# A three-block network in fp32 pairs: late low parts on GpSimd, two units' high products first, forget gate sums in the level loop

## The chip, the cores and the metric

One core of a Trainium2 chip runs one program. The metric is the device time of one execution in microseconds (us). Before: a median of 2212.71 us over 3 executions (2212.23 to 2213.28).

## What is computed

The input is one sequence of 512 tokens of width 1024. The first block is a token mixer of four recurrences and attentions, cross attention over 256 memory tokens and a gated network; two further layers follow. The change touches only the first mixer's beginning:

```python
xn = rmsnorm(x, norm_mix_pre)          # x * rsqrt(mean(x*x) + eps) * gain
proj = xn @ w_in + b_in                # 1024 -> 3592 columns
(m_q, m_k, m_v, m_o, m_i, m_f, ..., h_q, h_f, h_i, h_g) = split(proj)
# mlstm: log_f = log_sigmoid(m_f), g = cumsum(log_f), limits from i - g
# hgrn:  f = lb + (1-lb)*sigmoid(h_f), log_f = log f, g = cumsum(log_f),
#        attn[t,s] = sum_k q[t,k] exp(g[t,k]-g[s,k]) k[s,k]
```

## The kernel before

**Units.** Every matrix is cut into units of 128 output columns: 1024 x 128 weights, 512 KB, in a ring of four buffers (`raw`, `wh`, `wl`). For each unit SyncE's queue loads `raw`, ScalarE writes the rounded high part `wh` (L1377), GpSimd subtracts to get the low part `wl` in two halves (L523), and TensorE makes 24 products of 128x128 by 128x512: high by `xh`, high by `xl`, low by `xh` for each of the eight blocks of x. VectorE then empties the PSUM bank (`scaled`, L1951), which also applies the token norm. ScalarE adds the bias. `unit_split`, `unit_done` and `emptied` count these steps. ScalarE makes the high parts where the program text calls `raise_to(n)`, so what stands ahead of such a call delays the unit.

**The start.** ScalarE makes `xh` from the eight blocks of x (L1758), VectorE `xl` (`low`, L1951), and TensorE's first unit waits for each block of `xl` in turn. Before, the first four units go one at a time: 16 high products (L1103, L1104), then 8 low ones (L1110). Ahead of unit 1's low products stand the token sums of the norm (L680), which need the squares made by ScalarE (L1765) and added by VectorE (L2021, L2023). After unit 1 the inverse root is spread over the partitions (L698), and only then is unit 0's bank emptied. Units 4, 5 and 6 follow (L591 to L593); unit 4's high part waits for that first emptied bank, unit 6's comes after ScalarE's gate functions in `hgrn` (L1610 to L1617).

**The recurrence's levels.** `hgrn` works on two halves b of 128 channels. For each it runs seven levels and a diagonal: VectorE makes an argument (`level_argument`, L2235 and L2236), ScalarE its exponential (L1633), VectorE the operands (`level_operands`, L2241), TensorE the scores of all heads (16 small products, L1021) and then one whole unit (`fill`) to have work meanwhile. VectorE also copies the level's scores out (L2275) and empties the unit. VectorE's work in a level stands in this order: argument, scores of the level before, operands, emptying of the unit. The next scores wait for the operands.

**The forget gates.** These are rows of 4x512 for the other recurrence (`mlstm`). ScalarE takes a logarithm (`gate_logarithms`, L1538 to L1541), VectorE sums and bounds (`forget_sums`, `gate_rows_made`, `gate_limits`, L2142 to L2159, all ahead of the levels), TensorE turns the rows into columns (L983), and ScalarE copies the columns to `small` (L1649). Ahead of the levels TensorE waits for this copy (`take(cols_ready)`).

Of the kernel before, what the change touches and what calls it, by code (L numbers as in the profile page):

```python
# [30 lines left out]
P = 128  # L31
# [150 lines left out]
def build(nc, x_in, mem_in, w_in, par_in, con_in, moba_in, alibi_in, na_in, dist_in, out):  # L182
    with ExitStack() as ctx:
# [313 lines left out]
        @block.sync  # L497
        def _(sp):
            sp.dma_start(par[:], par_in).then_inc(inputs_in, 16)
            for b in (0, 2, 4, 5, 6, 7):  # L500
                sp.dma_start(x[:, b, :], x_in[:, b, :]).then_inc(x_in_sem[b], 16)
            for k in range(1, RING):
                sp.dma_start(raw[:, k, :], w_in[k * P:(k + 1) * P, :]).then_inc(unit_in[k], 16)
                if k == 1:
                    sp.dma_start(con[:, 0:EARLY_CONSTS], con_in[:, 0:EARLY_CONSTS]).then_inc(early_constants_in, 16)
            sp.dma_start(con[:, EARLY_CONSTS:], con_in[:, EARLY_CONSTS:]).then_inc(constants_in, 16)
            with sp.Fori(1, UNITS // RING) as i:
                for k in range(RING):

                    sp.wait_ge(unit_done, RING * i + (k + 1 - RING))  # L510
                    sp.dma_start(raw[:, k, :], w_in[bass.ds((RING * i + k) * P, P), :]).then_inc(unit_in[k], 16)
            for n in range(UNITS // RING * RING, UNITS):
                sp.wait_ge(unit_done, n + 1 - RING)
                sp.dma_start(raw[:, n % RING, :], w_in[n * P:(n + 1) * P, :]).then_inc(unit_in[n % RING], 16)


        @block.gpsimd
        def _(pool):
            def lower(k, high):
                pool.wait_ge(high_split, high)  # L520

                for half in (slice(0, KT * P // 2), slice(KT * P // 2, KT * P)):
                    m = pool.tensor_tensor(wl[:, k, half], raw[:, k, half], wh[:, k, half].bitcast(F32), ALU.subtract)  # L523
                m.then_inc(unit_split, 1)

            for w in weights:
                m = pool.memset(w, 0.0)
            m.then_inc(weights_cleared, 1)
            for n in range(RING):
                lower(n, n + 1)  # L530
            with pool.Fori(1, UNITS // RING) as i:  # L531
                for k in range(RING):
# [6 lines left out]
        def _(pe):  # L539
# [432 lines left out]
            def hgrn():  # L972
# [8 lines left out]
                take(gate_rows)  # L981
                for t in range(T):
                    m = pe.transpose(score_ps[:, 0, 4 * t:4 * t + 4], gate_b[0:4, t * P:(t + 1) * P], ident[0:4, 0:4])  # L983
                m.then_inc(cols_turned, 1)
                fill(FILL_START)
                take(copied_v, 2)
                take(cols_ready)
# [10 lines left out]
                for b in range(2):  # L998
# [10 lines left out]
                    for lev in range(len(LEVELS) + 1):  # L1009
# [14 lines left out]
                        if lev in FILL_LEVELS:  # L1024
                            fill()
                    if b == 0:

                        take(far_copied, 2)
# [84 lines left out]
            for n in range(4):  # L1113
                high_products(n, first_bank(n))
                if n == 1:
                    pe.wait_ge(early_constants_in, 16)
                    take(square_added, KT - 2)
                    token_sums(square_sum, True, False)
                    take(square_made, KT)
                    token_sums(sq[:, (KT - 1) % 2, :], False, True).then_inc(square_used, 2)  # L1120
                low_products(n, first_bank(n))
                if n == 1:
                    spread_tokens()
# [228 lines left out]
        def _(act):  # L1352
# [183 lines left out]
            def gate_logarithms():  # L1536
                f = slice(32, 36)
                step(act.activation(gate_a[f, :], gates[f, :], ACT.Abs))  # L1538
                step(act.activation(gate_a[f, :], gate_a[f, :], ACT.Exp, scale=-1.0))
                raise_to(5)  # L1540
                act.activation(gate_b[f, :], gate_a[f, :], ACT.Ln, bias=1.0).then_inc(gate_logs, 1)  # L1541

# [62 lines left out]
            def hgrn():  # L1605
                first = [(FIRST["in"] + 1 + i, b) for i, b in enumerate(FIRST_BLOCKS)]
                for n, b in first[0:2]:
                    add_bias(n, b)
                take(gate_arg)
# [8 lines left out]
                m.then_inc(gate_fun, 1)  # L1618
                for n, b in first[2:4]:
                    add_bias(n, b)  # L1620
# [27 lines left out]
                take(cols_turned)  # L1648
                act.activation(small[:, 32:48], score_ps[:, 0, 0:16], ACT.Identity).then_inc(cols_ready, 1)  # L1649
                for b in range(2):  # L1650
# [12 lines left out]
                    for lev in range(len(LEVELS)):  # L1663
                        if lev:
                            level()
                            raise_to(later_unit(FILL_START + len(FILL_LEVELS) * b + lev - 1) + 3)
                        if b == 0 and lev == len(LEVELS) - 1:
                            edges(1)
# [92 lines left out]
            raise_to(1)  # L1761
            for b in range(KT):
# [3 lines left out]
                if b == 4:  # L1766
                    raise_to(2)
# [7 lines left out]
            gate_logarithms()  # L1775
# [159 lines left out]
        def _(dve):  # L1935
# [265 lines left out]
            def hgrn():  # L2201
# [53 lines left out]
                forget_sums()  # L2255
                scaled(*first[5])
                gate_rows_made()
# [5 lines left out]
                gate_limits()  # L2263
# [3 lines left out]
                for b in range(2):  # L2267
# [11 lines left out]
                    for lev, half in enumerate(LEVELS):  # L2279
# [11 lines left out]
                        if lev - 1 in FILL_LEVELS:  # L2291
                            fill()
                    scores(6)
# [463 lines left out]
```

## Time and profile before

| | before |
|---|---|
| median of 3 executions | 2212.71 us |
| the profiled execution, its own time | 2214.52 us |
| its span, first to last instruction | 2212.7 us |
| TensorE busy | 2158.8 us, 98% |
| VectorE, ScalarE, GpSimd busy | 47%, 39%, 40% |
| mean granted clock of TensorE | 0.992 |

TensorE's busy time counts overlapping products and is modelled at their ends, so its 98% is read as "hardly ever without work", and gaps between starts of products are the better measure. A number behind `<-` names what ended an engine's idle time.

### The profile page before, as it was taken

Reading aid. Unit: us, or ns where it says so; the run is one execution under the profiler, and the core shown is the slowest. Engines: PE = TensorE matmul, PEld = TensorE weight load, DVE = VectorE, ACT = ScalarE, POOL = GpSimd, SP = SyncE. Lnnn points to the kernel's source line nnn. Section 1 sums busy time; section 2 is a strip of 40 time slices with the busy share of each in tenths; the row PEclk is TensorE's granted clock in tenths of the full one; section 3 lists DMA queues with packets and bytes.
Section 4 is the critical chain, followed back from the end, with each engine's and each line's share of the span. In section 5 each row is a group of like instructions: output and inputs, shape, how many; then the busy total and the mean of one; then the engine's idle time right before and its main releaser. Section 6 shows DMA issues by size and latency. Waiting matters only on the chain.

```text
span 2212.7 us, 28185 instructions
## 1 busy us (share of the span) xinstructions
PE 2158.8 (98%) x10422; PEld 1734.4 (78%) x10422; DVE 1050.6 (47%) x1526; ACT 852.5 (39%) x1281; POOL 891.3 (40%) x684
## 2 busy tenths in 40 slices
PE   8999999899999989998999999999999999999999
PEld 6875788688888868766888888888888877888887
DVE  5765646686626252476541321436733756323221
ACT  6435545532222243555442332434433344423221
POOL 5431245154444443210544444443333325444443
PEclk9999999999999999999999999999999999999999
DMA  4212123123323332101223222322222213222233
GB/s 165 77 60 83 39 85 106 39 95 119 109 95 98 107 128 77 58 30 37 88 97 102 96 95 95 112 78 80 72 86 77 76 48 105 95 96 95 97 100 99
DMA packets 54971, 193.42 MB, mean 87 GB/s; under 512 B 6096, under 2 KB 6352, under 8 KB 54480
## 3 DMA queue, kind: packets, MB, share of 16 engines
q1 hardware_dynamic: 49968, 180.54, 24.7%
q10 hardware_dynamic: 4896, 11.41, 1.6%
q8 instruction: 74, 1.21, 0.2%
q14 instruction: 33, 0.27, 0.0%
HBM read 189.82 MB, written 2.10 MB: 87 GB/s over the span
## 4 chain that ended last, share of the span: by engine, by line
issue 54%; POOL 28%; PE 17%; POOLq 1%; DVE 0%; DMA 0%; ACT 0%; SPq 0%; DVEq 0%; ACTq 0%
POOL wl L523 28%; PE gemm_ps L557 6%; PE gemm_ps L558 6%; PE gemm_ps L559 6%; DVE xl L1951 0%; POOLq L520 0%; DMA x<-x_in 0%; POOLq L531 0%; ACT xh L1758 0%; ACT wh L1377 0%; ACT sq L1765 0%; PE turn_ps L674 0%; DVE tmp L2023 0%; DVE tmp L2021 0%; DVE x L2047 0%
## 5 line engine op out<-in xcount | busy, mean ns | idle before, releaser
L523 POOL TENSOR_TENSOR wl<-raw,wh 128x512 fp32r<-128x512 f32 x678 | 887.6, 1332 | 1303.4 <-ACT wh L1377 1303.2
L1377 ACT ACTIVATE wh<-raw 128x1024 fp32r<-128x1024 f32 x339 | 358.8, 1059 | 743.3 <-DMA raw<-w_in 728.6
L557 PE MATMUL gemm_ps<-xh,wh 128*128 128x512 f32 x1200 | 475.9, 397 | 0.9 <-DVE arena L1951 0.9
L559 PE MATMUL gemm_ps<-xh,wl 128*128 128x512 f32 x1200 | 468.7, 391 | 0.0
L558 PE MATMUL gemm_ps<-xl,wh 128*128 128x512 f32 x1200 | 468.5, 390 | 0.0
L558 PE MATMUL gemm_ps<-arena_r,wh 128*128 128x512 f32 (+1 forms) x1088 | 417.2, 383 | 0.0
L557 PE MATMUL gemm_ps<-arena_r,wh 128*128 128x512 f32 (+1 forms) x832 | 320.1, 385 | 1.1 <-DVE x L2047 0.6
L559 PE MATMUL gemm_ps<-arena_r,wl 128*128 128x512 f32 (+1 forms) x832 | 317.5, 382 | 0.0
L557 PEld LDWEIGHTS gemm_ps<-xh,wh 128*128 128x128 f32 x1200 | 226.2, 188 | 52.0 <-issue 4.0
L558 PEld LDWEIGHTS gemm_ps<-xl,wh 128*128 128x128 f32 x1200 | 226.1, 188 | 48.8 <-issue 2.4
L559 PEld LDWEIGHTS gemm_ps<-xh,wl 128*128 128x128 f32 x1200 | 226.0, 188 | 47.5
L558 PEld LDWEIGHTS gemm_ps<-arena_r,wh 128*128 128x128 f32 x1088 | 205.1, 189 | 41.2 <-issue 1.4
L2047 DVE TENSOR_TENSOR x<-x,gemm_ps 128x512 f32<-128x512 f32 x84 | 57.8, 688 | 316.6 <-PE gemm_ps L559 304.6
L1951 DVE SCALAR_TENSOR_TENSOR arena<-gemm_ps,rstd 128x512 f32<-128x512 f32 (+1 forms) x116 | 85.2, 735 | 233.0 <-PE gemm_ps L559 189.3
L557 PEld LDWEIGHTS gemm_ps<-arena_r,wh 128*128 128x128 f32 x832 | 157.1, 189 | 34.1 <-issue 2.6
L559 PEld LDWEIGHTS gemm_ps<-arena_r,wl 128*128 128x128 f32 x832 | 157.1, 189 | 29.9
L1951 DVE SCALAR_TENSOR_TENSOR tmp<-gemm_ps,rstd 128x512 f32<-128x512 f32 x64 | 44.3, 692 | 207.1 <-PE gemm_ps L559 207.0
L591 PE MATMUL gemm_ps<-xh,wh 128*128 128x512 f32 x232 | 101.9, 439 | 12.1 <-DVE xl L1951 8.7
L557 PE MATMUL gemm_ps<-y_r,wh 128*128 128x512 f32 x256 | 100.0, 391 | 0.0
L559 PE MATMUL gemm_ps<-y_r,wl 128*128 128x512 f32 x256 | 99.6, 389 | 0.0
L2378 DVE TENSOR_TENSOR arena_r<-sq,arena_r 128x512 fp32r<-128x512 f32 x64 | 94.1, 1470 | 2.2
L593 PE MATMUL gemm_ps<-xh,wl 128*128 128x512 f32 x232 | 91.4, 394 | 0.0
(399 smaller groups left out, 2539.3 us busy)
## 6 DMA issues: line engine op xcount, KB each, us to landing
raw<-w_in SPq DMA_DIRECT2D x338, 512.0 KB, 3.5
arena<-na_in ACTq DMA_DIRECT2D x14, 256.0 KB, 2.7
out<-x ACTq DMA_DIRECT2D x8, 256.0 KB, 2.8
x<-x_in SPq DMA_DIRECT2D x6, 256.0 KB, 6.3
arena<-alibi_in ACTq DMA_DIRECT2D x6, 256.0 KB, 3.4
con<-con_in SPq DMA_DIRECT2D x1, 1424.0 KB, 11.5
arena<-moba_in ACTq DMA_DIRECT2D x1, 1024.0 KB, 5.1
arena<-mem_in ACTq DMA_DIRECT2D x1, 1024.0 KB, 4.7
```

Of the source, the lines that this page charges most:

```text
L523: m = pool.tensor_tensor(wl[:, k, half], raw[:, k, half], wh[:, k, half].bitcast(F32), ALU.subtract)
L557: pe.matmul(o, wh[:, n % RING, w], h[:, kt, 0:width], start=(kt == 0), stop=False)
L558: pe.matmul(o, wh[:, n % RING, w], l[:, kt, 0:width], start=False, stop=False)
L559: last = pe.matmul(o, wl[:, n % RING, w], h[:, kt, 0:width], start=False, stop=(kt == nkt - 1))
L591: pe.matmul(o, wh[:, n % RING, w], h[:, kt, :], start=(kt == 0), stop=False)
L593: m = pe.matmul(o, wl[:, n % RING, w], h[:, kt, :], start=False, stop=(kt == KT - 1))
L1377: act.activation(wh[:, k % RING, :], raw[:, k % RING, :], ACT.Copy).then_inc(high_split, 1)
L1951: done(dve.scalar_tensor_tensor(out=o, in0=a, scalar=scalar, in1=b, op0=op0, op1=op1), s)
L2047: done(dve.tensor_tensor(x[:, e, :], x[:, e, :], bank(n0, e), ALU.add), emptied)
L2378: done(dve.tensor_tensor(l[:, b, :], sq[:, b % 2, :], h[:, b, :].bitcast(F32), ALU.subtract), rhs_ready)
```

## The change

It has six parts. (1) GpSimd waits for six blocks of `xl` before its first subtraction. (2) SyncE's queue waits for the fourth unit's weights before it issues the load of the late constants. (3) TensorE does the high products of units 0 and 1, the low ones of both, the high ones of unit 2, then the norm's sums, and spreads the inverse root after unit 2's low products instead of unit 1's. (4) ScalarE makes the high parts of units 1 to 3 ahead of all the squares. (5) ScalarE's gate logarithm moves into `hgrn`, where its functions stand beside like ones. (6) VectorE's three gate steps stand behind the emptying in levels 1, 2 and 3 of the first half, the turning behind level 4's unit, ScalarE's copy in level 6, and the wait for it behind the levels.

```diff
             sp.dma_start(con[:, 0:EARLY_CONSTS], con_in[:, 0:EARLY_CONSTS]).then_inc(early_constants_in, 16)
+            sp.wait_ge(unit_in[RING - 1], 16)
             sp.dma_start(con[:, EARLY_CONSTS:], con_in[:, EARLY_CONSTS:]).then_inc(constants_in, 16)
...
             m.then_inc(weights_cleared, 1)
+            pool.wait_ge(rhs_ready, KT - 2)
             for n in range(RING):
                 lower(n, n + 1)
...
-            for n in range(4):
-                high_products(n, first_bank(n))
-                if n == 1:
-                    pe.wait_ge(early_constants_in, 16)
-                    take(square_added, KT - 2)
-                    token_sums(square_sum, True, False)
-                    take(square_made, KT)
-                    token_sums(sq[:, (KT - 1) % 2, :], False, True).then_inc(square_used, 2)
-                low_products(n, first_bank(n))
-                if n == 1:
-                    spread_tokens()
+            high_products(0, first_bank(0))
+            high_products(1, first_bank(1))
+            low_products(0, first_bank(0))
+            low_products(1, first_bank(1))
+            high_products(2, first_bank(2))
+            first_norm()
+            low_products(2, first_bank(2))
+            spread_tokens()
+            high_products(3, first_bank(3))
+            low_products(3, first_bank(3))
...
-            raise_to(1)
+            raise_to(3)
             for b in range(KT):
...
-                if b == 4:
-                    raise_to(2)
...
-            gate_logarithms()
...
                 for n, b in first[0:2]:
                     add_bias(n, b)
+                f = slice(32, 36)
+                step(act.activation(gate_a[f, :], gates[f, :], ACT.Abs))
+                step(act.activation(gate_a[f, :], gate_a[f, :], ACT.Exp, scale=-1.0))
...
                 m.then_inc(gate_fun, 1)
+                act.activation(gate_b[f, :], gate_a[f, :], ACT.Ln, bias=1.0).then_inc(gate_logs, 1)
...
+                        if b == 0 and lev == 6:
+                            take(cols_turned)
+                            act.activation(small[:, 32:48], turn_ps[:, 0, 0:16], ACT.Identity).then_inc(cols_ready, 1)
...
-                forget_sums()
                 scaled(*first[5])
-                gate_rows_made()
                 scaled(*first[6])
...
-                gate_limits()
...
                         if lev - 1 in FILL_LEVELS:
                             fill()
+                        if b == 0 and lev in (1, 2, 3):
+                            (forget_sums, gate_rows_made, gate_limits)[lev - 1]()
```

`first_norm` holds the six removed lines between `if n == 1:` and the low products.

**ScalarE from unit 5's high part to unit 6's.** Rows `4x512` are the gate logarithm; `small` is the other recurrence's bound; L1610 to L1617 (before) and L1618 to L1625 (now) are its exponential, sigmoid and logarithm. Before:

```order
L1538 ACTIVATE arena<-arena 4x512 [waits act_step]
L1539 ACT_TABLE_LOAD
L1539 ACTIVATE arena<-arena 4x512 [waits act_step]
L1377 ACTIVATE wh<-raw 128x1024 [waits unit_done,unit_in1,act_step]
L1541 ACT_TABLE_LOAD
L1541 ACTIVATE arena<-arena 4x512
L1528 ACTIVATE arena<-arena,par 128x512 [waits emptied] x2
L1610 ACT_TABLE_LOAD
L1610 ACTIVATE small<-small 128x2 [waits gate_arg]
L1613 ACT_TABLE_LOAD
L1613 ACTIVATE arena<-arena 128x512 [waits bias_added]
```

Now:

```order
L1389 ACTIVATE wh<-raw 128x1024 [waits unit_done,unit_in1]
L1540 ACTIVATE arena<-arena,par 128x512 [waits emptied]
L1615 ACTIVATE arena<-arena 4x512
L1616 ACT_TABLE_LOAD
L1616 ACTIVATE arena<-arena 4x512 [waits act_step]
L1618 ACTIVATE small<-small 128x2 [waits gate_arg,act_step]
L1621 ACT_TABLE_LOAD
L1621 ACTIVATE arena<-arena 128x512 [waits bias_added]
```

Two table loads are gone; the exponentials share one, and the gate's logarithm comes after the sigmoid's, ahead of unit 6's high part.

**VectorE in levels 1 to 3 of the first half.** L2248 are the operands, L1958 the emptying of the level's unit, L2242 and L2243 the next argument, L2279 the scores' copies (before: L2241, L1951, L2235 and L2236, L2275). Before:

```order
L2241 TENSOR_TENSOR sq<-arena 128x512 x2
L1951 SCALAR_TENSOR_TENSOR arena<-gemm_ps,rstd 128x512
L2235 TENSOR_TENSOR arena<-arena 128x16x16
L2236 TENSOR_TENSOR arena<-arena 128x16x16
L2275 COPY_PREDICATED y_all<-con,score_ps 128x4x128 x2
L2241 TENSOR_TENSOR tmp<-arena 128x512 x2
L1951 SCALAR_TENSOR_TENSOR arena<-gemm_ps,rstd 128x512
L2235 TENSOR_TENSOR arena<-arena 128x32x8
```

Now:

```order
L2248 TENSOR_TENSOR sq<-arena 128x512 x2
L1958 SCALAR_TENSOR_TENSOR arena<-gemm_ps,rstd 128x512
L2149 TENSOR_SCALAR arena<-arena 4x512
L2150 TENSOR_TENSOR arena<-arena 4x512
L2152 SCALAR_TENSOR_TENSOR arena<-arena 4x512
L2242 TENSOR_TENSOR arena<-arena 128x16x16
L2243 TENSOR_TENSOR arena<-arena 128x16x16
L2279 COPY_PREDICATED y_all<-con,score_ps 128x4x128 x2
L2248 TENSOR_TENSOR tmp<-arena 128x512 x2
L1958 SCALAR_TENSOR_TENSOR arena<-gemm_ps,rstd 128x512
L2157 COPY arena<-arena 4x512
L2159 TENSOR_TENSOR arena<-arena 4x512
```

The gate steps stand between a unit's emptying and the next level's argument, so that argument, the scores' copies and the operands all move back by their length.

## Rows read from the trace of the kernel before

**Rows 1.** The page: busy us (share of the span) xinstructions of each engine.
```profile
PE 2158.8 (98%) x10422; PEld 1734.4 (78%) x10422; DVE 1050.6 (47%) x1526; ACT 852.5 (39%) x1281; POOL 891.3 (40%) x684
```

**Rows 2.** Timeline of VectorE, 9 to 17 us: start, duration, engine, line, operation, tiles, count.
```profile
9.52 7.82 DVE L1951 SCALAR_TENSOR_TENSOR xl<-x,par,xh 128x512 fp32r<-128x512 f32 x6 [0.62 <-ACT xh L1758]
...
13.22 0.75 DVE L1951 SCALAR_TENSOR_TENSOR xl<-x,par,xh 128x512 fp32r<-128x512 f32 x1
```

**Rows 3.** Timeline of ScalarE, the eight high blocks' last six.
```profile
8.71 3.77 ACT L1758 ACTIVATE xh<-x,par 128x512 fp32r<-128x512 f32 x6
```

**Rows 4.** Timeline of TensorE, 17 to 25 us, [idle before <-releaser].
```profile
17.40 0.79 PE L1103 MATMUL gemm_ps<-xh,wh 128*128 128x512 f32 x1 [0.47 <-DVE xl L1951]
...
18.41 3.01 PE L1110 MATMUL gemm_ps<-xh,wl 128*128 128x512 f32 x8
21.26 0.39 PE L1103 MATMUL gemm_ps<-xh,wh 128*128 128x512 f32 x1
...
24.91 1.03 PE L680 MATMUL turn_ps<-con,tmp 128*128 128x4 f32 x8
```

**Rows 5.** Timeline of VectorE, the sums of squares.
```profile
21.77 3.00 DVE L2023 TENSOR_TENSOR tmp<-tmp,sq 128x512 f32<-128x512 f32 x2 [0.78 <-ACT sq L1765]
```

**Rows 6.** Timeline of TensorE: the spread of the norm, and unit 6's first product.
```profile
28.60 1.05 PE L698 MATMUL turn_ps<-con,eps 128*128 128x128 f32 x8
...
51.28 0.39 PE L591 MATMUL gemm_ps<-xh,wh 128*128 128x512 f32 x1
```

**Rows 7.** Timeline of ScalarE: high parts of units 4 and 6, gate functions between.
```profile
31.20 1.06 ACT L1377 ACTIVATE wh<-raw 128x1024 fp32r<-128x1024 f32 x1 [3.11 <-DVE arena L1951]
...
33.55 1.28 ACT L1539 ACT_TABLE_LOAD   x1
...
37.88 0.63 ACT L1541 ACTIVATE arena<-arena 4x512 f32<-4x512 f32 x1
...
46.23 1.04 ACT L1377 ACTIVATE wh<-raw 128x1024 fp32r<-128x1024 f32 x1
```

**Rows 8.** Timeline of VectorE (two scans) and of GpSimd (unit 6's second half).
```profile
47.37 4.52 DVE L2227 TENSOR_TENSOR_SCAN arena<-arena 128x512 f32<-128x512 f32 x2
...
48.60 2.21 POOL L523 TENSOR_TENSOR wl<-raw,wh 128x512 fp32r<-128x512 f32 x1
```

**Rows 9.** Timeline around 75 us: TensorE's first far products, ScalarE's copy of the gate columns.
```profile
75.28 0.17 ACT L1649 ACTIVATE small<-score_ps 128x16 f32<-128x16 f32 x1
...
75.54 0.90 PE L994 MATMUL turn_ps<-sq 64*128 64x128 f32 x6 [0.88 <-issue]
```

**Rows 10.** Stretches (A:B, length) with VectorE's busy us: the three gate steps.
```profile
57.60:60.01 2.41, 2.31 (x3) 1.00 0.64 212
60.74:64.42 3.68, 3.58 (x4) 1.00 0.04 10
72.77:73.93 1.16, 1.09 (x3) 1.00 0.00 0
```

**Rows 11.** Timeline of TensorE and VectorE in the level loop, 84 to 92 us.
```profile
84.60 1.16 PE L1021 MATMUL score_ps<-sq 64*128 64x128 f32 x16
...
91.36 1.16 PE L1021 MATMUL score_ps<-tmp 64*128 64x128 f32 x16
...
91.54 0.69 DVE L1951 SCALAR_TENSOR_TENSOR arena<-gemm_ps,rstd 128x512 f32<-128x512 f32 x1 [2.15 <-PE gemm_ps L559]
```

**Rows 12.** Timeline at 116 us: VectorE's level operands beside GpSimd's subtractions.
```profile
116.11 2.39 DVE L2241 TENSOR_TENSOR tmp<-arena 128x512 f32<-128x512 f32 x2
...
116.40 3.24 POOL L523 TENSOR_TENSOR wl<-raw,wh 128x512 fp32r<-128x512 f32 x2 [2.16 <-ACT wh L1377]
```

**Rows 13.** Timeline of TensorE: scores of the second half's levels 0 and 1.
```profile
134.17 2.08 PE L1021 MATMUL score_ps<-tmp 64*128 64x128 f32 x16 [1.02 <-ACT y_all L1662]
...
143.66 1.16 PE L1021 MATMUL score_ps<-sq 64*128 64x128 f32 x16
```

**Rows 14.** Stretches with busy us of each engine, then TensorE's granted clock (1.00 is 2.4 GHz), DMA.
```profile
120.00:140.00 20.00, 17.64 (x105) 13.72 (x104) 12.63 (x20) 5.77 (x12) 5.08 (x4) 0.83 0.15 50
```

More of the change, by code:

```diff
@@ L980, in hgrn @@
                     unit(FIRST["in"] + n, xh, xl)
[L981 to L984, printed above, removed]
                 fill(FILL_START)
                 take(copied_v, 2)
-                take(cols_ready)
                 def far(s, ps):
@@ L1025, in hgrn @@
                             fill()
+                        if b == 0 and lev == 4:
+                            take(far_copied, 2)
+                            take(gate_rows)
+                            for t in range(T):
+                                m = pe.transpose(turn_ps[:, 0, 4 * t:4 * t + 4], gate_b[0:4, t * P:(t + 1) * P],
+                                                 ident[0:4, 0:4])
+                            m.then_inc(cols_turned, 1)
                     if b == 0:
-                        take(far_copied, 2)
+                        take(cols_ready)
                         take(level_ready)
@@ L1111, in low_products, with first_norm @@
                 m.then_inc(unit_done, 1)
-            for n in range(4):
-                high_products(n, first_bank(n))
-                if n == 1:
-                    pe.wait_ge(early_constants_in, 16)
-                    take(square_added, KT - 2)
-                    token_sums(square_sum, True, False)
-                    take(square_made, KT)
-                    token_sums(sq[:, (KT - 1) % 2, :], False, True).then_inc(square_used, 2)
-                low_products(n, first_bank(n))
-                if n == 1:
-                    spread_tokens()
+            def first_norm():
+                pe.wait_ge(early_constants_in, 16)
+                take(square_added, KT - 2)
+                token_sums(square_sum, True, False)
+                take(square_made, KT)
+                token_sums(sq[:, (KT - 1) % 2, :], False, True).then_inc(square_used, 2)
+            high_products(0, first_bank(0))
[8 more added lines that the diff above has]
+            low_products(3, first_bank(3))
             blocks_split[0] += KT
@@ L1534, in fill @@
                     filled[0] += 1
[L1536 to L1541, printed above, removed]
             def copy_attended(b):
@@ L1647, in hgrn @@
                     add_bias(n, b)
-                take(cols_turned)
-                act.activation(small[:, 32:48], score_ps[:, 0, 0:16], ACT.Identity).then_inc(cols_ready, 1)
                 for b in range(2):
```

## The prediction, made before the changed kernel had run

> **What bounds it now.** The page comes first: TensorE is busy for 2158.8 of 2212.7 us, the next engine for less than half [rows 1]. So only three things can change the time: TensorE's waits, its clock, and the number of its products, which stays. Then the timeline, place by place where the change works. At the start the blocks of `xl` set the pace: a block takes VectorE 0.75 us alone (the block at 13.22), yet the last six take 7.82 us [rows 2], because GpSimd subtracts beside them. TensorE gets the last block at 17.40 us, and its next eight products start in 2.85 us (18.41 to 21.26), 0.36 us each, where 16 later ones take 3.65 us, 0.228 us each [rows 4]; the slower pace is that of the 1.2 GHz level (512 columns in 0.43 us), the quicker that of 2.4 GHz. From 26 to 75 us it never waits; it then idles 0.88 us until ScalarE's copy of the gate columns at 75.28 us [rows 9]. In the levels it doesn't wait: the scores come every 6.76 us, and VectorE sits idle 2.15 us before it empties a unit [rows 11].
>
> **The sum, part by part.** Times are those of the trace of before; S is the start of the norm's spread, 28.60 us before [rows 6].
>
> *Start: `xl`.* With GpSimd held until six blocks are there, each takes 0.75 us and a gap of 0.04. ScalarE delivers `xh` faster than that, the last at 12.48 us [rows 3]. From 9.52 us [rows 2] blocks three to six then end near 12.7; the seventh has begun when GpSimd starts; the eighth waits behind one subtraction, and I give it 0.9 more, a little over what the sums of squares show (1.50 us each beside GpSimd [rows 5], against 0.75 for a like pass alone). It ends near 15.1 instead of 17.34: 2.2 us.
>
> *Start: order.* TensorE then runs without gaps from 9.5 us, so I expect the 2.4 GHz level by 16 us. Unit 1's high products follow at 16.1; the low ones of units 0 and 1 and the high ones of unit 2 add 3.65 + 3.62 + 3.65 us: the norm's sums stand at 27.0 us. The squares now start after three high parts, near 16 us, and their sums run beside GpSimd's eight subtractions: first add at 17.1, six adds at about 1.5 us [rows 5] and 0.6 us for a square, ready at 26.0 to 26.6 us. No wait, with 0.4 us to spare. Sums to spread is 3.69 us as before (24.91 to 28.60) [rows 4, 6], so S = 30.7, 2.1 us later. But two units' worth of products fewer lie behind it: high and low of unit 2 are 24 products, 5.44 us. Unit 6 was reached S + 22.68 [rows 6] and now could be at S + 17.24 = 47.9 us, 3.4 us earlier.
>
> *Unit 6's low part.* Here the next thing is late. ScalarE starts unit 4's high part at S + 2.60 and unit 6's 15.03 us later [rows 7]; without two table loads of 1.28 us it is 12.4: S + 15.0, so GpSimd asks at S + 16.1, behind the high part's 1.04 us. VectorE's first scan began 1.14 us after unit 6's high part (47.37 against 46.23) [rows 7, 8]; now the gate's logarithm of 0.63 us [rows 7] lies ahead of the high part and not of the scan, so the scan starts at S + 15.5: it is first. Before, two scans and two subtractions of this place took turns: 4.52 us for the scans, 2.21 us for the second half instead of some 1.28 [rows 8]. So now: scan (1.2 us, half of 4.52 less a turn of 1.05), half, scan, half, each handed over a tenth early, to S + 20.1. Unit 6 starts at 50.8 us, not at 51.28: of 3.4 us 0.5 is left. Bounds: 2.0 us where the scans don't hold GpSimd up, -0.3 where the norm's sums come late by 0.8.
>
> *Wait for the gate columns.* It falls away: VectorE's 7.25 us of gate steps [rows 10] no longer stand ahead of the operands, and the copy isn't waited for. Next in line are the far operands, by the same lengths ready some 2.7 us ahead (an estimate). -0.9 us. The turning itself only moves: nothing.
>
> *Gate steps in the levels.* VectorE's slack there: it finishes the operands at 91.54 - 2.15 = 89.39, TensorE wants them at 91.36 [rows 11]: 1.97 us. Level 1 gets 2.41 us [rows 10]: 0.44 us over. And the delay moves the operands into GpSimd's time. What that costs is seen once, at 116 us [rows 12]: begun 0.29 us ahead of GpSimd, the two operands took 2.39 us, not 1.42. The same steps lie between argument and operands, and between argument and GpSimd's start (exponential, high part), once the weights have landed; in levels 1 to 3 as they run now GpSimd comes only after the operands. So 0.44 + 0.97 and a little: 1.45 us. Level 2 gets 3.68 us, in which a subtraction ran beside GpSimd; 2.7 us alone. VectorE begins only with the delayed operands done and can't catch up, as its own 4.6 us of a level (6.76 - 2.15) and 2.7 make 7.3, 0.5 over, and 1.0 for GpSimd: 1.5 us. Level 3 gets 1.16 us: 0.3 us. From level 4 on the slack is back. Together +3.3 us; bounds 1.1 (no contention) and 3.9 (level 3 pays in full).
>
> *At nothing:* the late load of constants (first needed when VectorE empties the first fill unit, at 74 us); ScalarE's later squares (above); its column copy in level 6 (needed after level 7).
>
> Sum: -0.5 - 0.9 + 3.3 = **+1.9 us**. Against the profiled execution's own 2214.52 us (span 2212.7) this is 2216.4; against the median, 1.8 us lower, **2214.6 us**. A measurement of this kernel can tell about 0.2%, 4.4 us, from no change: the bounds are 2208.3 and 2217.1. So I forecast no change that can be told.
>
> **A rule weighed.** At 116 us VectorE, begun first, had its first operand undisturbed and paid once [rows 12]. The Trainium skill ("SBUF — State Buffer", section "Who interferes with whom") says that a VectorE instruction with two SBUF inputs and a GpSimd one that reads SBUF exclude each other, and that whoever issues first has the port for the whole instruction. By it the smallest head start is as good as the 0.29 us there, and lost, it would cost a second turn: rival 3. The rows of the level loop have no case of it.
>
> **Rivals.**
>
> 1. *The slack holds.* The level steps cost their bare excess, 1.1 us, as VectorE's idle time and TensorE's steady 6.76 us [rows 11] suggest, and the scans cost less. For: GpSimd's start hangs on a ScalarE step that a later argument moves too. Against: that is what happened at 116 us [rows 12]. -2.0 - 0.9 + 1.1 = -1.8: 2210.9 us.
>
> 2. *Slower: the clock falls in the levels.* Between 120 and 140 us the granted clock was 0.83, part of the time at the 1.2 GHz level [rows 14]: after a wait of 1.02 us that had followed another one shortly before, the scores of level 0 stood 9.49 us ahead of the next instead of 6.76 [rows 11, 13]. That is 2.73 us. Now two waits of 1.5 us, 8 us apart, stand in levels 2 and 3. One wait of 0.88 us, without a second, didn't lower the clock [rows 9]. It decides if a wait of 1.5 us alone is enough: 2214.6 + 2.7 = 2217.3 us, over the bound.
>
> 3. *GpSimd gets in first.* By the rule above, as a mechanism here: were the subtraction to begin just ahead of the operands of levels 2 and 3, each of the two operands waits behind a half: two turns, not one, in each of two levels, about 1.5 us more in each (2.39 - 1.42 and half a microsecond for the longer wait): +3.0: 2217.6 us.
>
> 4. *The fall after 131 us goes away.* The waits there depend on TensorE's own weighted sums and ScalarE's copies, untouched, but the clock need not fall the same: 2214.6 - 2.7 = 2211.9 us.
>
> 5. *The start keeps its gain and the levels too*, both contentions wrong and the clock better: -3.4 - 0.9 - 2.7 = 2205.7 us.
>
> **Chances.** Forecast 0.46; rival 1 0.24; rival 2 0.12; rival 3 0.05; rival 4 0.09; rival 5 0.04. The range reaches from rival 1, with part of rival 4 in it, to rivals 2 and 3: 2209.6 to 2218.2 us. Faster than 2208.3 is rival 5, 0.04; slower than 2217.1 are rivals 2 and 3 less a part in which other terms come out better, 0.13; the rest, 0.83, is the same.
>
> **What would show it.** After the change: blocks of `xl` of 0.75 us with the last ending near 15 us; GpSimd's first subtraction near 12.8 us; TensorE's sums of the norm near 27 us without a wait; a wait on GpSimd's low part of some 3 us ahead of unit 6; no wait at the first far product; waits of TensorE on VectorE's operands ahead of the scores of levels 2 and 3 of 1.5 us each, the operands 2.4 us for two there. Right in sign but wrong in size if the operands take 1.4 us. The forecast is wrong if the levels show no wait at all, if unit 6 isn't waited for, or if the granted clock falls in a stretch where it was 1.00.

## The result, and the profile after

The changed kernel took 2217.34 us (median), the kernel before, run beside it, 2213.85 us: a ratio of 1.0015, with a 95% interval from 1.0010 to 1.0021. By the ratio that is 3.3 us or 0.15% more (3.5 us between the two medians), within the 0.2% that the prediction counted as no change, 2.7 us above its figure and inside its range. Of these 2.7 us, 1.1 are the kernel before, which stood at 2212.71 us when the forecast was made. The sign is that of the forecast; how far its steps hold is another question, and the profiled execution (own time 2217.46 us, span 2215.7) seems to say that one of them was far off.

The start first. Timelines of the changed kernel, each with start, duration, engine, line, operation, tiles: VectorE's seventh and eighth block of `xl`, GpSimd's first subtractions, and unit 6's high part on ScalarE.

```profile
12.67 1.88 DVE L1958 SCALAR_TENSOR_TENSOR xl<-x,par,xh 128x512 fp32r<-128x512 f32 x1
...
14.58 1.66 DVE L1958 SCALAR_TENSOR_TENSOR xl<-x,par,xh 128x512 fp32r<-128x512 f32 x1
...
12.71 13.15 POOL L524 TENSOR_TENSOR wl<-raw,wh 128x512 fp32r<-128x512 f32 x8 [8.42 <-DVE xl L1958]
...
48.03 1.06 ACT L1389 ACTIVATE wh<-raw 128x1024 fp32r<-128x1024 f32 x1
```

And TensorE, down to its first far products:

```profile
14.60 0.50 PE L1108 MATMUL gemm_ps<-xh,wh 128*128 128x512 f32 x1 [0.60 <-DVE xl L1958]
...
16.29 0.50 PE L1108 MATMUL gemm_ps<-xh,wh 128*128 128x512 f32 x1 [0.96 <-DVE xl L1958]
...
17.25 0.63 PE L1109 MATMUL gemm_ps<-xl,wh 128*128 128x512 f32 x1
...
29.35 0.84 PE L682 MATMUL turn_ps<-con,tmp 128*128 128x4 f32 x7
...
32.99 1.05 PE L700 MATMUL turn_ps<-con,eps 128*128 128x128 f32 x8
...
52.90 0.50 PE L593 MATMUL gemm_ps<-xh,wh 128*128 128x512 f32 x1 [2.40 <-POOL wl L524]
...
54.81 0.63 PE L594 MATMUL gemm_ps<-xl,wh 128*128 128x512 f32 x1
...
77.48 0.93 PE L991 MATMUL turn_ps<-sq 64*128 64x128 f32 x6
```

The seventh block began 0.04 us ahead of GpSimd and took 1.88 us; the last ended at 16.24 us, where the blocks of before ended at 17.34 [rows 2]. TensorE, already at the 2.4 GHz level, waited twice and then stood at the 1.2 GHz level from 17.25 to 20.23 us (products 0.43 us apart). So the norm's sums stand at 29.35 us and its spread at 32.99 us instead of 28.60 [rows 6]. Unit 6 comes after a wait of 2.40 us, at 52.90 us instead of 51.28 [rows 6], and behind it the products are 0.43 us apart again. The far products don't wait any more ([rows 9] had 0.88 us).

Now the levels: TensorE's scores of levels 1 to 5, VectorE's operands of levels 1 to 3, GpSimd's subtractions beside them.

```profile
86.59 1.16 PE L1018 MATMUL score_ps<-sq 64*128 64x128 f32 x16
94.81 1.16 PE L1018 MATMUL score_ps<-tmp 64*128 64x128 f32 x16 [1.39 <-DVE tmp L2248]
103.05 1.16 PE L1018 MATMUL score_ps<-sq 64*128 64x128 f32 x16 [1.41 <-DVE sq L2248]
110.08 1.16 PE L1018 MATMUL score_ps<-tmp 64*128 64x128 f32 x16 [0.18 <-DVE tmp L2248]
117.19 1.16 PE L1018 MATMUL score_ps<-sq 64*128 64x128 f32 x16
...
92.38 2.37 DVE L2248 TENSOR_TENSOR tmp<-arena 128x512 f32<-128x512 f32 x2
...
100.63 2.37 DVE L2248 TENSOR_TENSOR sq<-arena 128x512 f32<-128x512 f32 x2
...
107.64 2.40 DVE L2248 TENSOR_TENSOR tmp<-arena 128x512 f32<-128x512 f32 x2
...
92.77 3.11 POOL L524 TENSOR_TENSOR wl<-raw,wh 128x512 fp32r<-128x512 f32 x2 [5.86 <-ACT wh L1389]
100.74 3.39 POOL L524 TENSOR_TENSOR wl<-raw,wh 128x512 fp32r<-128x512 f32 x2 [4.85 <-ACT wh L1389]
107.74 3.42 POOL L524 TENSOR_TENSOR wl<-raw,wh 128x512 fp32r<-128x512 f32 x2 [3.61 <-ACT wh L1389]
```

Against the steady 6.76 us of [rows 11] the distances are 8.22, 8.24 and 7.03 us: 1.46 + 1.48 + 0.27 = 3.2 us, where the prediction had 3.3. The next distance, 7.11 us, holds the turning that the change puts there.

Last the clock, by stretches: length, busy us and count of TensorE, its weight loads, VectorE, ScalarE, GpSimd, then the granted clock (1.00 is 2.4 GHz), DMA share and GB/s.

```profile
0.00:20.00 20.00, 9.59 (x24) 7.00 (x25) 12.23 (x20) 13.04 (x19) 11.04 (x11) 0.92 0.82 295
20.00:40.00 20.00, 20.00 (x101) 16.78 (x100) 10.24 (x10) 6.80 (x11) 9.13 (x7) 0.99 0.24 81
40.00:60.00 20.00, 17.60 (x71) 13.98 (x70) 12.49 (x17) 17.42 (x26) 11.46 (x9) 0.91 0.25 79
...
80.00:100.00 20.00, 18.61 (x113) 14.99 (x112) 15.67 (x23) 7.15 (x12) 6.00 (x4) 1.00 0.18 64
100.00:120.00 20.00, 18.40 (x115) 14.53 (x114) 17.11 (x24) 6.41 (x9) 9.35 (x6) 1.00 0.24 79
120.00:140.00 20.00, 17.64 (x120) 13.63 (x120) 11.22 (x20) 9.04 (x21) 5.14 (x4) 0.99 0.15 54
140.00:160.00 20.00, 20.00 (x113) 16.13 (x112) 11.93 (x18) 5.56 (x8) 5.67 (x5) 0.92 0.17 54
```

Before, every stretch up to 120 us had 1.00 and the one from 120 to 140 us 0.83 [rows 14]. A stretch of 20 us at 0.91 is 1.8 us lost, so the profile after has lost 1.6 + 0.2 + 1.8 = 3.6 us to the clock by 60 us and lost less than before from 120 to 160 us (1.8 against 3.4). One profile of each kernel can't say whether that belongs to the change. Two quantities are used from here on to keep it apart:

- **Without the clock:** the span times its mean granted clock, averaged over all timed runs of a kernel. It counts a microsecond at the 1.2 GHz level as half of one. The kernel before gives 2194.2, 2194.4 and 2194.1 us in its three sets of runs, and 2194.2 is used as its value throughout; the changed one gives 2196.9 us, +2.7 us, with a mean clock of 0.9916 against 0.9918 (some 0.5 us). The standard error of such an average over eleven runs is 0.2 to 0.7 us, mostly about 0.5; that of their mean clock is 0.0002 to 0.0005, or 0.5 to 1.1 us.
- **Position:** in the one profile, the time from TensorE's first product to the first half's value products (128.14 - 8.86 = 119.28 us before; 133.51 - 8.86 = 124.65 us after), less what the clock cost by then. After: +5.37 - 3.6 = +1.8 us.

Both take a low stretch for time lost in full, which it need not be. The granted clock doesn't count the low level at the very start, where the products are 0.43 us apart under a clock of 1.00. It lasted to some 20 us in the profile before, to 17 and 15 us in those of `e1_levels_only` and `e11_turning_only`, the same program up to there; yet all three have the norm's sums 16.04 or 16.05 us behind the first product, the last two after waiting 1.32 us for them. There the lower level filled a wait and cost nothing.

### The profile page after: what moved, and what is told of

The parts are those of the page before. It is cut to its first block, busy times and chain, and to the rows that moved or that the text cites. A ratio compares the mean times of both kernels' runs of the same rounds, so it can differ in the third digit from the quotient of the medians.

```text
span 2215.7 us, 28187 instructions
## 1 busy us (share of the span) xinstructions
PE 2159.4 (97%) x10422; PEld 1735.9 (78%) x10422; DVE 1051.0 (47%) x1526; ACT 850.5 (38%) x1279; POOL 893.3 (40%) x684
## 4 chain that ended last, share of the span: by engine, by line
issue 54%; POOL 28%; PE 17%; POOLq 1%; ACT 0%; DMA 0%; DVE 0%; SPq 0%; DVEq 0%; ACTq 0%
POOL wl L524 28%; PE gemm_ps L559 6%; PE gemm_ps L560 6%; PE gemm_ps L561 6%; POOLq L521 0%; DMA x<-x_in 0%; POOLq L533 0%; ACT xh L1768 0%; ACT wh L1389 0%; PE turn_ps L676 0%; DVE xl L1958 0%; DVE x L2054 0%; SPq L499 0%; DVEq L2053 0%; ACTq L1767 0%
## 5 line engine op out<-in xcount | busy, mean ns | idle before, releaser
L1958 DVE SCALAR_TENSOR_TENSOR arena<-gemm_ps,rstd 128x512 f32<-128x512 f32 (+1 forms) x116 | 85.2, 735 | 240.7 <-PE gemm_ps L561 194.0
L1958 DVE SCALAR_TENSOR_TENSOR tmp<-gemm_ps,rstd 128x512 f32<-128x512 f32 x64 | 44.3, 692 | 207.0 <-PE gemm_ps L561 206.9
```

The source lines that it names most:

```text
L1958: done(dve.scalar_tensor_tensor(out=o, in0=a, scalar=scalar, in1=b, op0=op0, op1=op1), s)
```

## The experiments

Theory A, from the traces: the levels are what was forecast; the start is the mis-sized step, by the tie at block seven (VectorE's seventh block and GpSimd's first subtraction begin almost together), and what the clock does behind its waits comes on top. Theory B: the start gained what was forecast, and the levels cost more. All runs were timed beside the kernel before. The last two columns are in us against the kernel before, as defined above; a position is that of one profile.

| run | median us | ratio, 95% | mean clock | without the clock | position |
|---|---|---|---|---|---|
| changed kernel | 2217.34 | 1.0015 (1.0010, 1.0021) | 0.9916 | +2.7 | +1.8 |
| e1_levels_only | 2213.62 | 0.9999 (0.9990, 1.0008) | 0.9930 | +2.4 | +1.8 |
| e2_start_only | 2212.18 | 0.9996 (0.9987, 1.0005) | 0.9925 | +0.3 | -1.2 |
| e3_all_eight | 2217.34 | 1.0013 (1.0004, 1.0022) | 0.9913 | +2.0 | +1.2 |
| e4_raise_six | 2211.02 | 0.9991 (0.9982, 1.0000) | 0.9935 | +1.1 | -0.5 |
| e5_spread | 2214.89 | 1.0002 (0.9993, 1.0011) | 0.9915 | +0.5 | +1.3 |
| e6_all_three | 2209.78 | 0.9982 (0.9972, 0.9991) | 0.9924 | -1.8 | -2.9 |
| e7_six_spread | 2210.09 | 0.9978 (0.9969, 0.9987) | 0.9934 | -0.8 | -2.0 |
| e8_six_blocks_only | 2215.23 | 1.0001 (0.9992, 1.0010) | 0.9910 | -0.7 | -0.2 |
| e9_steps_ahead | 2208.88 | 0.9981 (0.9972, 0.9990) | 0.9925 | -3.4 | -3.8 |
| e10_steps_ahead_eight | 2210.20 | 0.9984 (0.9975, 0.9993) | 0.9920 | -3.8 | -4.5 |
| e11_turning_only | 2210.91 | 0.9993 (0.9984, 1.0002) | 0.9926 | -0.4 | -1.3 |

### The change in two halves

`e1_levels_only` is the kernel before with the change's later hunks: the gate steps called after levels 1 to 3, the turning after level 4, ScalarE's column copy in level 6.

> The kernel before with only the later part of the change: the three gate steps inside levels 1 to 3, the turning of the gate rows after level 4, its wait gone from ahead of the far products. Theory A (the start was the step mis-sized, the levels were priced rightly): the same waits ahead of levels 2, 3 and 4 as in the changed kernel, 1.4 + 1.4 + 0.2 us, 3.2 us in all, less the 0.9 us wait for the gate columns: +2.3 us against the kernel before, or about +1.1 if the part of the clock fall that was given back near 140 us comes with these waits. Theory B (the start gained what was forecast and the rest is the levels): all of the 3.3 us measured plus the 0.5 us of the start, +3.8 us.

`e2_start_only` is the kernel before with the other hunks: GpSimd's wait, the held-back constants, TensorE's order, `raise_to(3)`, the gate logarithms beside the others.

> The kernel before with only the earlier part of the change: GpSimd waiting for six blocks, the late constants' transfer held back, TensorE's new order, the four early weight copies, the gate logarithms beside the others. Theory A: the seventh and eighth block still take 1.9 and 1.7 us, TensorE runs at the lower clock from 17 to 20 us, the norm is spread near 33.0 us and unit 6 waits 2.4 us for its low part, followed by the lower clock for some 3 us: the end of the first products is 3.4 us later than before, and the whole +1 to +3.4 us (by what a shorter clock fall later gives back). Theory B: -0.5 us, as forecast.

The later half has the same waits ahead of levels 2 and 3, 1.40 us each, and stands at +1.8 us by position and +2.4 us without the clock: theory A. The earlier half isn't what theory A said of it. Its profile has the tie and the wait ahead of unit 6, but no low level at the start. TensorE's spread of the norm and unit 6 in it, and the stretch around:

```profile
31.14 1.05 PE L700 MATMUL turn_ps<-con,eps 128*128 128x128 f32 x8
...
51.05 0.79 PE L593 MATMUL gemm_ps<-xh,wh 128*128 128x512 f32 x1 [2.40 <-POOL wl L524]
...
40.00:60.00 20.00, 17.60 (x76) 14.22 (x75) 16.76 (x22) 15.88 (x25) 11.54 (x8) 0.91 0.20 70
```

Counted from each profile's first product (8.59 us here, 8.86 before), unit 6 comes at 42.46 us against 42.42 before: the start is worth nothing, not -0.5, and not +3.4 either. Behind unit 6 the far products don't wait for the gate columns, which is most of the 1.2 us by which the half is better by position. But TensorE came to them 1.8 us later for the clock, 0.66 us after ScalarE's copy of these columns (75.35 us), so whether the new order alone frees it isn't shown. Nearly all of what the profile after shows at the start (unit 6 1.6 us late, another 1.8 us behind it) is the clock; the second of these falls is in this profile too. In medians the halves are -0.7 and -2.2 us and the whole is +3.5; without the clock they are +2.4 and +0.3, and the whole is +2.7, where they add up within their errors. By position they don't (+1.8 and -1.2 against +1.8): each half's profile lacks the 0.88 us wait for the gate columns, which the whole can lose only once.

### The seventh block

`e3_all_eight` is the changed kernel with one line changed:

```
-            pool.wait_ge(rhs_ready, KT - 2)
+            pool.wait_ge(rhs_ready, KT)
```

> The changed kernel with GpSimd waiting for all eight blocks instead of six, so that no block of VectorE's can meet a subtraction of GpSimd's. Theory A (blocks 7 and 8 slowed by GpSimd, 1.1 us each, cause the two waits and with them the clock fall from 17 to 20 us): the blocks take 0.75 us each, the last ends at 14.2 us, TensorE has no wait there and stays at the higher clock, the norm is spread at 30.7 to 31.5 us instead of 33.0; but unit 6's low part hangs on the same chain of ScalarE, so that only -1.6 to -3 us against the changed kernel remain. Rival C (the low parts, now 1.5 us later, become the bound, or the clock falls anyhow): 0 to +1 us against the changed kernel.

VectorE's last three blocks, and TensorE's norm sums and unit 6, in that run:

```profile
11.63 2.33 DVE L1958 SCALAR_TENSOR_TENSOR xl<-x,par,xh 128x512 fp32r<-128x512 f32 x3
...
27.02 1.02 PE L682 MATMUL turn_ps<-con,tmp 128*128 128x4 f32 x8 [0.79 <-DVE tmp L2030]
...
53.53 0.50 PE L593 MATMUL gemm_ps<-xh,wh 128*128 128x512 f32 x1 [2.21 <-POOL wl L524]
...
20.00:40.00 20.00, 19.21 (x83) 16.13 (x82) 10.68 (x11) 6.54 (x10) 8.97 (x7) 0.83 0.26 82
```

The blocks do end at 13.96 us, 0.78 us each, and TensorE has neither wait there. But the gain hoped for, -1.6 to -3 us, is 0.0 in the median and -0.8 us without the clock: rival C. The next limit is VectorE's sums of squares, which TensorE reaches 0.79 us too early, and behind that wait the clock fell (0.83). The tie at block seven is real and cost at most 1.1 us. What taking it away gives back is seen in three pairs of kernels (this run, `e6_all_three` against `e7_six_spread`, `e10_steps_ahead_eight` against `e9_steps_ahead`): 0.8, 1.0 and 0.4 us without the clock, each good to 0.6 to 0.9 us, and 0.6, 0.9 and 0.7 us by position.

`e8_six_blocks_only` looks at the same limit from the other side: the kernel before with only the two waits (`pool.wait_ge(rhs_ready, KT - 2)` and the one on SP).

> The kernel before with nothing but GpSimd's wait for six blocks and the late constants' transfer held back. Theory H (VectorE's blocks are ahead of GpSimd's subtractions until the sixth): the last block ends near 16 us instead of 17.3, but the norm sums wait about 2.4 us instead of 1.3 for VectorE's sums of squares, so that the norm and unit 6 stay where they were: 0 +- 0.5 us. Rival I (TensorE's order and not the blocks held the start): unit 1 and the norm come 1.1 us earlier and the gain is -1 us.

```profile
24.92 0.84 PE L682 MATMUL turn_ps<-con,tmp 128*128 128x4 f32 x5 [2.51 <-DVE tmp L2025]
```

From its first product at 8.80 us that is 16.12 us, before it was 16.05 [rows 4], with 2.51 us of waiting: theory H, no gain. In the order of before, the sums of squares set the norm's time whatever the blocks do. The median is 0.35 us above that of the kernel before.

### Unit 6

`e4_raise_six` is the changed kernel with one more call:

```
                 for n, b in first[0:2]:
                     add_bias(n, b)
+                raise_to(6)
                 f = slice(32, 36)
```

> The changed kernel with ScalarE's weight copy of unit 6 moved ahead of the gate functions, from 48.0 to about 41.5 us. Theory A: GpSimd has the low part ready by 46 us, the 2.4 us wait ahead of unit 6 goes, TensorE stays at the higher clock behind it: -2.4 us, and with the clock fall up to -4 us against the changed kernel. Rival D (the wait only moves: the gate functions and scans are 1.1 us later, so that the copies for units 7 and 8 or the far products' operands are waited for instead): -1 us or less, with a new wait of 1 us or more between 50 and 78 us.

ScalarE's high part, GpSimd's work on units 4 to 6, and the stretch:

```profile
39.28 1.05 ACT L1389 ACTIVATE wh<-raw 128x1024 fp32r<-128x1024 f32 x1
...
36.52 7.54 POOL L524 TENSOR_TENSOR wl<-raw,wh 128x512 fp32r<-128x512 f32 x6 [11.36 <-ACT wh L1389]
...
40.00:60.00 20.00, 20.00 (x94) 16.61 (x93) 12.76 (x18) 17.69 (x27) 10.95 (x9) 1.00 0.32 107
```

GpSimd is done with unit 6 at 44.06 us, where it was nearly 52.9, and TensorE is busy for the whole stretch: theory A. By position the gain against the changed kernel is 2.3 us, the wait of 2.40; without the clock it is 1.7 us. In medians it is 6.3 us, and the rest is the mean clock: 0.9935 against 0.9916, times 2212 us, is 4.2 us. No wait of 1 us took its place.

### The gate steps, spread or ahead

`e5_spread` cuts the two scans out as functions of their own and changes the call:

```
-                        if b == 0 and lev in (1, 2, 3):
-                            (forget_sums, gate_rows_made, gate_limits)[lev - 1]()
+                        if b == 0 and 1 <= lev < 6:
+                            (forget_sums, forget_scan, gate_rows_made, maximum_scan, gate_limits)[lev - 1]()
```

> The changed kernel with the same seven gate operations in five levels instead of three: two small ones (1.1 us) in level 1, a scan (1.2) in level 2, two (1.3) in level 3, a scan (1.2) in level 4, two (1.3) in level 5. Theory E (a level has 1.97 us to spare on VectorE; GpSimd, met earlier than before, adds 0.95 us to the operands): 1.1 to 1.3 + 0.95 us against 1.97 leaves waits of 0.1 to 0.3 us each, 1 us at most in all, where the changed kernel has 1.4 + 1.4 + 0.2 = 3.0: -2 to -3 us against the changed kernel in the time that doesn't hang on the clock. Rival F (what delays TensorE is the sum of the operations and not how they are spread): the waits add up to 3 us again and the time stays.

VectorE's operands of level 1, the scan and the operands of level 2, and the two longest of TensorE's waits:

```profile
89.20 1.42 DVE L2253 TENSOR_TENSOR tmp<-arena 128x512 f32<-128x512 f32 x2
...
92.33 2.10 DVE L2154 TENSOR_TENSOR_SCAN arena<-arena 4x512 f32<-4x512 f32 x1
...
96.93 2.38 DVE L2253 TENSOR_TENSOR sq<-arena 128x512 f32<-128x512 f32 x2
...
99.37 0.83 PE L1018 MATMUL score_ps<-sq 64*128 64x128 f32 x10 [1.11 <-DVE sq L2253]
...
121.08 1.16 PE L1018 MATMUL score_ps<-tmp 64*128 64x128 f32 x16 [0.78 <-DVE tmp L2253]
```

Without the clock this is -2.2 us against the changed kernel, as expected, but by position only -0.5, and its three waits (1.11, 0.18 and 0.78 us) add up to 2.1 us, not to 1 at most. The reason stands in the rows. With 1.1 us of gate steps ahead of them the operands of level 1 keep their 1.42 us; then the scan itself meets GpSimd and takes 2.10 us instead of 1.22, and the next operands 2.38. A step put in front can move the ones behind it into GpSimd's time. It isn't a matter of length alone: behind 1.33 us of steps the next operands took 2.39 us, behind the second scan, of 1.45 us, they took 1.42 us, and behind the last two steps (1.64 and 0.41 us) 2.39 us again. So what a level can hold isn't 1.97 us but what leaves the order of the two engines as it was.

`e7_six_spread` has this and unit 6's earlier high part, `e6_all_three` the wait for eight blocks as well.

> The changed kernel with both repairs: unit 6's weight copy ahead of the gate functions, and the gate operations over five levels. If the two waits are independent, the gains add: -1.7 (unit 6) and -2 to -3 (levels) against the changed kernel without the clock, some 3 us less than the kernel before with it. Rival G (the levels' slack is used up by the one repair): no more than either alone.

> As the run with both repairs, and GpSimd waiting for all eight blocks. Theory: as there; the wait for eight blocks takes 1.1 us of waiting for blocks 7 and 8 away, puts a wait of 0.8 us for the sums of squares in its place, so that it differs from the run with both repairs by less than 1 us where the clock is the same. Rival: with unit 6's wait gone the start gains the 1.7 us that the eight blocks end earlier.

They are 0.22% and 0.18% faster than the kernel before and 7 us below the changed one. The gains of the two repairs add without the clock (3.5 us for 1.7 and 2.2) and by position (3.8 us for 2.3 and 0.5, and more), against rival G; in the ratios of the timed runs the second adds 0.13% to the 0.24% of the first, with intervals that overlap. The mean clocks of two pairs go together: with the wait ahead of unit 6 they are 0.9916 and 0.9915 (changed, `e5_spread`), the same two kernels without it stand at 0.9935 and 0.9934. The eight blocks give another 1.0 +- 0.9 us without the clock, and nothing in the median: the profile of `e6_all_three` has a wait of 1.36 us ahead of the norm's sums and a clock of 0.91 in the stretch from 20 to 40 us, and its mean clock is 0.9924.

`e9_steps_ahead` leaves the gate steps where they stood before (so without the change's last two hunks) and keeps the rest with `raise_to(6)`; `e10_steps_ahead_eight` adds the wait for eight blocks.

> The changed kernel with unit 6's weight copy ahead of the gate functions and the seven gate operations back on VectorE ahead of the levels, where they stood before; only the turning of their rows stays after level 4. Theory (ahead of the levels VectorE has some 2 us to spare before the far products, in the levels it has not): no wait ahead of levels 1 to 7 of the first half, none ahead of unit 6, no wait for the gate columns: without the clock 3 to 4 us less than the changed kernel, some 2209 us. Rival (with TensorE 2.4 us earlier at the far products, VectorE's operands, ready at about 71.8 us, are now late): a new wait of 1 us or more ahead of the far products, and no better than the run with the gate operations spread over five levels.

> The same with GpSimd waiting for all eight blocks. Theory: the pair of runs before this one gave 0.9 us without the clock for that step; here as much or less, -0.5 +- 0.5 us against the run with six blocks. Rival: TensorE, 1 us earlier at the far products, waits for VectorE's operands: 0.

TensorE and VectorE in levels 1 to 3 of `e9_steps_ahead`, and its clock there:

```profile
80.44 1.16 PE L1018 MATMUL score_ps<-sq 64*128 64x128 f32 x16
87.20 1.16 PE L1018 MATMUL score_ps<-tmp 64*128 64x128 f32 x16
...
91.02 1.42 DVE L2249 TENSOR_TENSOR sq<-arena 128x512 f32<-128x512 f32 x2
...
80.00:100.00 20.00, 20.00 (x121) 15.95 (x120) 14.94 (x22) 6.92 (x9) 9.26 (x8) 1.00 0.24 79
100.00:120.00 20.00, 20.00 (x123) 16.02 (x122) 13.82 (x22) 8.26 (x15) 7.06 (x7) 1.00 0.23 79
```

The levels are 6.76 us apart again, the operands take 1.42 us, TensorE is busy throughout and waits nowhere from 17 us to the value products at 124.14 us. That is the best median, 2208.88 us, 4.9 us under the kernel before and 8.5 under the changed one. Its interval overlaps that of `e7_six_spread`, which it leads by 2.6 us without the clock. The eight blocks add 0.4 us without the clock, as expected, and the median is 1.3 us higher: not told apart.

`e11_turning_only` is the kernel before with nothing but the turning, its copy and its wait moved.

> The kernel before with only the turning of the gate rows, its copy and its wait moved from ahead of the far products to after level 4; the gate operations themselves stay where they were. Forecast's term: the 0.88 us wait goes and nothing takes its place: -0.9 us. Rival (ScalarE's copy of unit 6's neighbour, not the gate columns, ended that wait): 0 to -0.3 us, and a gap of the same length in the same place.

By position it gains 1.3 us (the 0.88 us wait, and some of what stood around it), without the clock 0.4 +- 0.5 us. The forecast's -0.9 lies between, and its first far products at 73.61 us have no gap ahead of them.

## Why the prediction was right, and where it was not

- **The blocks of `xl`: wrong.** "The seventh has begun when GpSimd starts" is the step that failed, in what it was taken to mean, a block undisturbed. It had begun, by 0.04 us, and still took 1.88 us instead of 0.75: the last block ended at 16.24 us, not 15.1. The eighth, with 1.66 us, is as forecast (0.75 + 0.9).
- **The order and the norm: right once corrected.** In `e2_start_only`, where the clock held, the spread comes 22.55 us behind the first product, on the time axis of before 31.4 us, against 30.7 forecast. The 1.1 us of block seven is more than the difference, as the forecast had given TensorE 0.4 us too much from the last block to the sums (11.9 us; 27.49 - 15.96 = 11.53 in `e2_start_only`). The adds are at their limit, as the 0.4 us to spare said: with the last block 2.0 us earlier behind the first product than after the change (`e3_all_eight`) TensorE waits 0.79 us for them.
- **Unit 6's low part: right.** Forecast at 20.1 us behind the spread; 52.90 - 32.99 = 19.91 us, and 19.91 in `e2_start_only`. ScalarE's high part came at S + 15.04 (forecast 15.0). The wait ahead of unit 6 was 2.40 us. The two scans and the two halves of the low part took turns in the order given (scans at 48.40 and 49.66 us, halves at 49.17 and 50.67). So the start was worth 0.0 us where -0.5 was forecast: 1.1 us for the seventh block, less 0.4 and 0.2 where later terms had too much.
- **The wait for the gate columns: right.** Gone; 0.9 forecast, 0.4 (without the clock) and 1.3 (position) in `e11_turning_only`.
- **The levels: right, size and cause.** 3.2 us for 3.3, level by level 1.46, 1.48 and 0.27 for 1.5, 1.5 and 0.3; the operands took 2.37, 2.37 and 2.40 us. `e1_levels_only` shows it alone, `e9_steps_ahead` shows it gone. Rival 1, the bare excess of 1.1 us, is out; so is rival 3, since VectorE began its operands ahead of GpSimd in all three levels, by 0.39, 0.11 and 0.10 us, and paid one turn in each.
- **The clock: not forecast where it fell.** Rival 2 had it fall in the levels; the granted clock stayed at 1.00 there with two waits of 1.4 us 8 us apart, in all four profiles that have them (changed kernel, `e1_levels_only`, `e3_all_eight`, `e4_raise_six`). Rival 4 came half true: the stretches after 120 us lost 1.8 us, not 3.4. What no rival had is a fall behind the wait ahead of unit 6, of which the prediction only said that "some 3 us" of waiting would stand there. It should have been given a price: in the pair of the changed kernel and `e4_raise_six`, taking that wait away was worth 2.3 us by position and 4.2 +- 0.9 us of mean clock.

The sum of the forecast was +1.9 us; the measure that leaves the clock out gives +1.8 by position and +2.7 over all runs. The rest of the +3.3 us is the clock and the uncertainty of either. That the sum fits so well by position is in part luck: the start came out 0.5 us worse than its term and the wait for the gate columns 0.4 us better.

## What to carry to other kernels

A kernel whose TensorE is busy 98% of its time changes by waits of one or two microseconds, and a single profile mixes them with the clock's changes of level, here up to 3.6 us in the first 60 us of 2216. Multiply every run's span by its mean clock and average before a cause is named, and compare the places of the same product in two profiles. Before work is put into an engine's idle time, look at what the instructions behind it will then run beside: of the five levels of `e5_spread`, each with 1.97 us of slack on VectorE and 1.1 to 2.1 us of small steps, two kept their operands clear of GpSimd and three didn't. How GpSimd is started matters too: a wait for six of eight blocks sets it off at the very moment at which VectorE goes on to the seventh. And ask of each weight part on the way to a wait whether it stands behind work that nobody waits for: one earlier copy on ScalarE gave more than the whole change had cost.

## What the runs showed of the hardware

**A near tie is no head start.** The block that began at 12.67 us, 0.04 us ahead of GpSimd's first subtraction at 12.71, took 1.88 us for 0.75. The Trainium skill ("SBUF — State Buffer", section "Who interferes with whom") says that whoever issues first has the port for the whole instruction. By that the block would have been undisturbed; at 0.04 us the trace doesn't agree; at 0.10, 0.11 and 0.39 us in the levels it does, where the first of the two operands took 0.69 us each time and only the second waited, as at 0.29 us before the pair paid once [rows 12]. The tie is no accident: GpSimd's wait ends with block six, when VectorE goes on to block seven, and in all seven profiles with the wait for six blocks the two begin 0.04 or 0.05 us apart. Whether the trace's start is the moment at which an instruction takes the port isn't shown, so the rule may hold and the recorded order mislead.

**Small instructions are held up too.** A scan of 4 partitions by 512 took 1.22 us alone and 2.10 us beside GpSimd, and a VectorE subtraction of that shape 0.68 us alone and 1.67 us beside it (before, at 61.47 us), though they move next to nothing. What these rows show is a wait of up to one GpSimd instruction, whatever the size of one's own.

**The same wait, another clock.** Ahead of the norm's sums `e1_levels_only` and `e11_turning_only`, which are the same program up to there, both waited 1.32 us. First a row of each, then the stretch of each:

```profile
24.42 1.03 PE L680 MATMUL turn_ps<-con,tmp 128*128 128x4 f32 x8 [1.32 <-DVE tmp L2027]
20.00:40.00 20.00, 18.68 (x88) 15.48 (x87) 6.57 (x9) 11.07 (x15) 10.25 (x8) 0.91 0.25 79
```

```profile
24.47 1.03 PE L680 MATMUL turn_ps<-con,tmp 128*128 128x4 f32 x8 [1.32 <-DVE tmp L2027]
20.00:40.00 20.00, 18.68 (x95) 15.58 (x95) 6.61 (x9) 12.66 (x17) 10.58 (x8) 1.00 0.23 79
```

In the first the clock fell behind it, in the second it held. Of the six profiles with a wait ahead of the norm's sums (0.79 to 2.51 us) five show a fall behind it. The wait ahead of unit 6 was followed by a fall in the changed kernel and in `e2_start_only` (2.40 us each), but not in `e3_all_eight` (2.21 us) nor in `e5_spread`, whose stretch from 40 to 60 us has 1.00 behind a wait of 2.42 us:

```profile
52.68 0.50 PE L593 MATMUL gemm_ps<-xh,wh 128*128 128x512 f32 x1 [2.42 <-POOL wl L524]
...
40.00:60.00 20.00, 17.58 (x82) 14.34 (x81) 13.20 (x18) 17.77 (x27) 11.45 (x9) 1.00 0.27 82
```

The Trainium skill ("TensorE: Matmul & The Clock Gate", Part 1) says of the rise to the higher level that its place varies from run to run of one kernel. The starts of the profiles before and of `e1_levels_only` agree (some 20 and 17 us for one program), and the rows above show as much for the fall. So a wait has a chance of a fall, not a fall; for the wait ahead of unit 6 the two pairs of kernels with and without it put its average at some 4 us of clock, each pair good to about 1 us. What stays open is why the halves of the change stood at a higher mean clock (0.9930 and 0.9925) than either whole kernel. `e2_start_only` has the wait ahead of unit 6 and the kernel before has not, and its clock is no lower (0.9925 +- 0.0005 against 0.9918). The level also falls far from the change: between 260 and 280 us the granted clock was 0.91 in the profiles before, of `e3_all_eight` and of `e5_spread`, and 1.00 in the profile after and those of the halves. So the 6 us by which the whole lies above the sum of its halves in the medians (+3.5 against -0.7 and -2.2) can't be laid on one place.
